# RWKV head norms: gate products made in the loop of the sums, and folded into the bonus and the heads

## The reference, cut to what matters

```python
g = jax.nn.sigmoid(xg @ g1) @ g2
...
mu = jnp.mean(y, axis=-1, keepdims=True)
var = jnp.mean(jnp.square(y - mu), axis=-1, keepdims=True)
y = ((y - mu) * lax.rsqrt(var + GN_EPS)).reshape(B, L, C)
y = y * ln_w.astype(f32) + ln_b.astype(f32)
bonus = jnp.sum(rh * kh * r_k.astype(f32), axis=-1, keepdims=True) * vh
y = y + bonus.reshape(B, L, C)
return (y.astype(h.dtype) * g) @ w_out
```

## Time and profile before

| | |
|---|---|
| median of 3 runs | 2298.06 us (2298.04 to 2304.33) |
| profiled execution, its own time | 2299.16 us |
| its span, first to last instruction | 2297.3 us |
| TensorE busy in the span | 2215.3 us (96%) |
| mean granted TensorE clock | 0.968 of full speed |
| VectorE, ScalarE, GpSimd busy | 1073.1, 804.6, 528.3 us |

### The profile page before, as it was taken

How to read it: one execution, slowest core, us unless ns; L and a number is a source line. 1 busy time by engine, 2 the same in 40 slices (tenths; PEclk the granted TensorE clock), 3 DMA queues, 4 the chain that set the end, 5 groups by cost and what they waited for, 6 DMA issues and landing times.

```text
span 2297.3 us, 50981 instructions
## 1 busy us (share of the span) xinstructions
PE 2215.3 (96%) x22812; PEld 1875.8 (82%) x22812; DVE 1073.1 (47%) x1480; ACT 804.6 (35%) x1388; POOL 528.3 (23%) x661
## 2 busy tenths in 40 slices
PE   7999998999899999899999999999998999999997
PEld 6888887877799955788888888888887668888886
DVE  5433325767566554743342463342274537433323
ACT  4333313574233341433332253332142324433320
POOL 2111103420233232621110331111162116211103
PEclk9999999999899997999999999999999779999999
DMA  4323321310000011232232132233123012323311
GB/s 159 129 93 117 118 79 56 113 67 19 13 4 4 4 56 70 102 107 96 93 130 91 56 108 96 93 113 127 56 70 106 1 37 74 111 93 114 130 51 37
DMA packets 28953, 183.42 MB, mean 80 GB/s; under 512 B 3216, under 2 KB 8144, under 8 KB 9792
## 3 DMA queue, kind: packets, MB, share of 16 engines
q1 hardware_dynamic: 27888, 178.79, 22.2%
q0 software_dynamic: 848, 1.37, 0.3%
HBM read 174.31 MB, written 4.30 MB: 78 GB/s over the span
## 4 chain that ended last, share of the span: by engine, by line
PE 87%; DVE 6%; POOL 3%; ACT 2%; issue 1%; DMA 0%; SPq 0%; POOLq 0%; ACTq 0%; DVEq 0%
PE psum L288 69%; PE psum L1603 6%; POOL h L348 1%; PE psum L1594 1%; PE psum L2470 1%; PE psum L2469 1%; PE psum L2456 1%; PE psum L363 1%; PE psum L1627 1%; POOL x L399 1%; DVE arena L340 1%; DVE split L263 1%; PE psum L1981 1%; PE psum L2301 1%; PE psum L1980 1%
## 5 line engine op out<-in xcount | busy, mean ns | idle before, releaser
L288 PE MATMUL psum<-x,split 128*128 128x256 f16 (+1 forms) x5568 | 642.6, 277 | 7.6 <-POOL x L399 6.1
L288 PEld LDWEIGHTS psum<-x,split 128*128 128x128 f16 x5568 | 544.9, 98 | 102.3 <-issue 16.0
L696 POOL TENSOR_TENSOR arena<-arena 128x256 f16<-128x256 f32 (+1 forms) x176 | 120.0, 682 | 772.7 <-ACT arena L545 772.7
L288 PE MATMUL psum<-x,split_more 128*128 128x256 f16 (+1 forms) x2496 | 288.2, 277 | 1.5 <-DVE x L2568 1.5
L288 PE MATMUL psum<-x,arena 128*128 128x256 f16 (+2 forms) x2448 | 281.9, 276 | 1.4 <-POOL x L947 1.2
L288 PEld LDWEIGHTS psum<-x,split_more 128*128 128x128 f16 x2496 | 245.8, 98 | 38.4 <-issue 1.9
L288 PEld LDWEIGHTS psum<-x,arena 128*128 128x128 f16 (+1 forms) x2448 | 240.7, 99 | 37.0 <-POOL x L947 2.5
L263 DVE SCALAR_TENSOR_TENSOR split<-stage,split 128x2048 f16<-128x2048 f32 (+1 forms) x77 | 190.5, 2474 | 161.1 <-ACT split L257 161.1
L288 PE MATMUL psum<-arena,split 128*128 128x256 f16 (+1 forms) x2304 | 260.9, 275 | 0.0
L288 PEld LDWEIGHTS psum<-arena,split 128*128 128x128 f16 x2304 | 225.0, 98 | 34.5 <-issue 2.2
L623 DVE SCALAR_TENSOR_TENSOR arena<-psum,arena 128x256 f32<-128x256 f32 (+1 forms) x176 | 75.4, 429 | 321.0 <-ACT arena L539 316.3
(11 more groups left out here) (217 smaller groups left out, 2652.6 us busy)
## 6 DMA issues: line engine op xcount, KB each, us to landing
stage<-in_w_gu SPq DMA_DIRECT2D x88, 1024.0 KB, 4.9
stage<-in_w_down SPq DMA_DIRECT2D x32, 1408.0 KB, 6.1
stage<-in_w_rkv SPq DMA_DIRECT2D x12, 1024.0 KB, 4.9
stage<-in_w_out SPq DMA_DIRECT2D x4, 1024.0 KB, 4.8
stage<-in_w_q SPq DMA_DIRECT2D x4, 1024.0 KB, 4.7
stage<-in_w_o SPq DMA_DIRECT2D x4, 1024.0 KB, 5.7
h_spill<-h SPq DMA_DIRECT2D x1, 2112.0 KB, 12.0
h<-h_spill SPq DMA_DIRECT2D x1, 2112.0 KB, 8.7
```

The lines of the kernel that those rows point to most:

```text
L288: last = pe.matmul(o, wt(wp, k), xs(xp, k), start=(k == 0 and wp == 0 and xp == 0), stop=(k == tiles - 1 and wp == 1))
L696: e.tensor_tensor(hid[s][:, 1, m, 0:n], hid32[:, no % 2, 0:n], hid[s][:, 0, m, 0:n], ALU.subtract).then_inc(hid_lo, 1)
```

## The change

The gates of all 16 tiles are made in the loop of the sums, ahead of bonus(i). As soon as tile i - 1 has its bonus and its square, DVE makes (bonus + ln_b) times gate and y times ln_w times gate (`with_gate`). What is left behind the inverse is one product and one sum (`normed`). FIRST = 11: from tile 11 on, the loop of the sums also makes inverse(i - 11) and normed(i - 11), so five tiles of half 0 are finished in the loop and three behind it. `inverted(1)` moves behind the norms of half 0. `split_hi` and `split_lo` of jobs[0] move forward to tiles 4 and 5; those of jobs[1] move behind the norms of half 0; those of jobs[2] and jobs[3] go between the groups of norms of half 1. The DMA that brings h back is cut in two: three quarters once all gates are made, the last quarter where it was; `s_back` is waited for at 32.

```diff
--- before.py
+++ after.py
@@ -833,7 +833,7 @@
                         beside.gpsimd(e, j)
                     sums(j, 0)
                 if beside:
-                    e.wait_ge(s_back, 16)
+                    e.wait_ge(s_back, 32)
                 add_h(e, T_out, 0)
                 sums(0, 1)
                 sums(1, 1)
@@ -1451,8 +1451,10 @@
                 gated.sync(e)
                 o.sync(e)
 
+                gated.gates_done(e)
+                e.dma_start(hflat[:, 0:6 * L], spill[:, 0:6 * L]).then_inc(s_back, 16)
                 gated.second.ready(e, KT - 1)
-                e.dma_start(hflat, spill).then_inc(s_back, 16)
+                e.dma_start(hflat[:, 6 * L:KT * L], spill[:, 6 * L:KT * L]).then_inc(s_back, 16)
 
             def act(e):
                 k_act(e)
@@ -1921,8 +1923,9 @@
             b_act, b_pool, b_pe, bon_dve = (sem(n) for n in ("rk_scaled", "rk_products", "bonus_sums", "bonus"))
             mean_pe, yc_dve, sq_act, var_pe = (sem(n) for n in ("y_means", "y_centred", "y_squares", "y_variances"))
             sd_act, sd_dve = sem("y_deviations"), sem("y_inverses")
-            gate_pe, iv_pe, yn_dve, y1_dve = (sem(n) for n in ("out_gates", "inverses_spread", "y_normed", "y_with_bonus"))
-            z_dve, z_act, z_pool = (sem(n) for n in ("gated", "gated_high", "gated_rest"))
+            gate_pe, bong_dve, yg_dve = (sem(n) for n in ("out_gates", "bonus_gated", "y_gated"))
+            iv_pe, yn_dve, z_dve, z_act, z_pool = (sem(n) for n in ("inverses_spread", "gated_normed", "gated_sums",
+                                                                     "gated_high", "gated_rest"))
 
             def t(arr, s, k):
                 a, m = HALF[s]
@@ -1958,44 +1961,52 @@
                     e.matmul(psum[0:HEADS, 4 + s, 0:width(s)], c("pick")[:, p0:p0 + HEADS], ysq[:, i % 2, 0:width(s)],
                              start=(k == 0), stop=(k == KT - 1)).then_inc(var_pe, 1)
 
+                def gate(i):
+                    s, k = tiles[i]
+                    a, m = HALF[s]
+                    if i >= 2:
+                        e.wait_ge(yg_dve, i - 1)
+                    e.matmul(at(i, 6 + i % 2), g2_sb[:, 0, k * P:(k + 1) * P], sgate[:, 0, a:a + m], start=True, stop=False)
+                    e.matmul(at(i, 6 + i % 2), g2_sb[0:GLO, 1, k * P:(k + 1) * P], sgate[0:GLO, 1, a:a + m], start=False,
+                             stop=True).then_inc(gate_pe, 1)
+
                 mean(0)
                 mean(1)
                 for i in range(2 * KT):
+                    gate(i)
                     bonus(i)
                     variance(i)
                     if i + 2 < 2 * KT:
                         mean(i + 2)
-                for i in range(KT):
-                    gate(e, i)
+                    if i >= FIRST:
+                        inverse(e, i - FIRST)
+                for i in range(2 * KT - FIRST, KT):
                     inverse(e, i)
 
-            def gate(e, i):
-                s, k = tiles[i]
-                a, m = HALF[s]
+            FIRST = 11
+
+            def inverse_bank(i):
                 if i >= KT:
-                    e.wait_ge(z_dve, i)
-                elif i >= 2:
-                    e.wait_ge(z_dve, i - 1)
-                o = at(i, 6 + i % 2 if s == 0 else 6)
-                e.matmul(o, g2_sb[:, 0, k * P:(k + 1) * P], sgate[:, 0, a:a + m], start=True, stop=False)
-                e.matmul(o, g2_sb[0:GLO, 1, k * P:(k + 1) * P], sgate[0:GLO, 1, a:a + m], start=False,
-                         stop=True).then_inc(gate_pe, 1)
+                    return 6 + i % 2
+                return 4 if i < 2 * KT - FIRST else i % 2
 
             def inverse(e, i):
                 s, k = tiles[i]
                 a, m = HALF[s]
                 e.wait_ge(sd_dve, s + 1)
-                if s == 0:
-                    if i >= 2:
-                        e.wait_ge(yn_dve, i - 1)
-                    else:
-                        e.wait_ge(bon_dve, 2 * KT)
-                e.matmul(at(i, i % 2 if s == 0 else 7), spreads[:, k * P:(k + 1) * P], sd[:, a:a + m], start=True,
+                if i == 2 * KT - FIRST:
+                    e.wait_ge(bon_dve, 2 * KT)
+                if i == KT:
+                    e.wait_ge(yg_dve, 2 * KT)
+                if 0 < i < 2 * KT - FIRST:
+                    e.wait_ge(yn_dve, i)
+                elif i % KT >= 2:
+                    e.wait_ge(yn_dve, i - 1)
+                e.matmul(at(i, inverse_bank(i)), spreads[:, k * P:(k + 1) * P], sd[:, a:a + m], start=True,
                          stop=True).then_inc(iv_pe, 1)
 
             def second_pe(e, q):
                 if q % 4 == 0 and q // 4 < KT:
-                    gate(e, KT + q // 4)
                     inverse(e, KT + q // 4)
 
             def act(e):
@@ -2026,14 +2037,16 @@
                     if i + 2 < 2 * KT:
                         scaled(i + 2)
                     square(i)
+                    if i == 4:
+                        split_hi(e, jobs[0])
                     if i == 8:
                         deviation(0)
-                    if i == 10:
-                        split_hi(e, jobs[0])
+                    if i >= FIRST + 1:
+                        high(e, i - FIRST - 1)
                 deviation(1)
+                for i in range(2 * KT - FIRST - 1, KT):
+                    high(e, i)
                 split_hi(e, jobs[1])
-                for i in range(KT):
-                    high(e, i)
                 split_hi(e, jobs[2])
 
             def high(e, i):
@@ -2057,45 +2070,53 @@
                     e.wait_ge(sd_act, s + 1)
                     e.reciprocal(sd[:, a:a + m], sd[:, a:a + m]).then_inc(sd_dve, 1)
 
+                def with_gate(i):
+                    s, k = tiles[i]
+                    y, bon, g = t(y_all, s, k), t(v_all, s, k), at(i, 6 + i % 2)
+                    e.wait_ge(gate_pe, i + 1)
+                    e.wait_ge(bon_dve, i + 1)
+                    e.scalar_tensor_tensor(out=bon, in0=bon, scalar=v("ln_b", k), in1=g, op0=ALU.add,
+                                           op1=ALU.mult).then_inc(bong_dve, 1)
+                    e.wait_ge(sq_act, i + 1)
+                    e.scalar_tensor_tensor(out=y, in0=y, scalar=v("ln_w", k), in1=g, op0=ALU.mult,
+                                           op1=ALU.mult).then_inc(yg_dve, 1)
+
                 for i, (s, k) in enumerate(tiles):
                     e.wait_ge(mean_pe, i + 1)
                     e.scalar_tensor_tensor(out=t(y_all, s, k), in0=at(i, 2 + i % 2), scalar=-1.0 / HD, in1=t(y_all, s, k),
                                            op0=ALU.mult, op1=ALU.add).then_inc(yc_dve, 1)
+                    if i:
+                        with_gate(i - 1)
                     e.wait_ge(b_pe, i + 1)
                     e.tensor_tensor(t(v_all, s, k), at(i, i % 2), t(v_all, s, k), ALU.mult).then_inc(bon_dve, 1)
+                    if i == 5:
+                        split_lo(e, jobs[0])
                     if i == 9:
                         inverted(0)
-                    if i == 11:
-                        split_lo(e, jobs[0])
-                for i in range(KT):
+                    if i >= FIRST:
+                        normed(e, i - FIRST)
+                with_gate(2 * KT - 1)
+                for i in range(2 * KT - FIRST, KT):
                     normed(e, i)
-                    if i == 1:
-                        inverted(1)
-                    if i == 3:
-                        split_lo(e, jobs[1])
-                split_lo(e, jobs[2])
+                inverted(1)
+                split_lo(e, jobs[1])
 
             def normed(e, i):
                 s, k = tiles[i]
-                yk, bon = t(y_all, s, k), t(v_all, s, k)
+                y, bon = t(y_all, s, k), t(v_all, s, k)
                 e.wait_ge(iv_pe, i + 1)
-                e.tensor_tensor(yk, yk, at(i, i % 2 if s == 0 else 7), ALU.mult).then_inc(yn_dve, 1)
+                e.wait_ge(yg_dve, i + 1)
+                e.tensor_tensor(y, y, at(i, inverse_bank(i)), ALU.mult).then_inc(yn_dve, 1)
                 e.wait_ge(yn_dve, i + 1)
-                e.scalar_tensor_tensor(out=bon, in0=yk, scalar=v("ln_w", k), in1=bon, op0=ALU.mult,
-                                       op1=ALU.add).then_inc(y1_dve, 1)
-                e.wait_ge(y1_dve, i + 1)
                 if i >= 3:
                     e.wait_ge(z_pool, i - 2)
-                e.wait_ge(gate_pe, i + 1)
-                e.scalar_tensor_tensor(out=zz[:, i % 3, 0:width(s)], in0=bon, scalar=v("ln_b", k),
-                                       in1=at(i, 6 + i % 2 if s == 0 else 6), op0=ALU.add, op1=ALU.mult).then_inc(z_dve, 1)
+                e.tensor_tensor(zz[:, i % 3, 0:width(s)], y, bon, ALU.add).then_inc(z_dve, 1)
 
             def second_dve(e, j):
                 if j < 2:
                     for i in range(4 * j, 4 * j + 4):
                         normed(e, KT + i)
-                if j == 0:
```

(12 more changed lines are left out.)

## The result

| | before | after |
|---|---|---|
| median | 2298.65 us (2298.04 to 2304.33, 5 runs) | 2287.22 us (2281.46 to 2289.36, 5 runs) |
| ratio, 95% interval | | 0.995, 0.9935 to 0.9964 |
| profiled execution | 2299.16 us, span 2297.3 | 2287.22 us, span 2285.3 |
| stage, from the first head mean to the eviction of out(3, 0) | 101.6 us | 90.4 us (820.2 to 910.6) |

The change is 11.4 us faster; 14.7 were forecast. A second set of runs of the same kernel gave 2286.99 against 2298.30, again 11.3. The profiled stage is shorter by 11.2, so nearly all of the difference arises in it: of the rest, the first head mean comes 1.6 us later in this profile, and what stands behind the stage takes 2.4 us less.

What follows compares the result with a forecast made beforehand. TensorE, 87% of the chain, bounds the kernel, mostly losing to half clock. Stage: 76.1 + 0.2 + 1.6 + 4.7 + 0.5 + 3.8 = 86.9 us against 101.6, 14.7 less: median 2283.4, range 2277.5 to 2290.5.

Steps and rivals of the forecast that it cites:

- The likeliest case: Whole kernel: the forecast itself, 14.7 us less, median 2283.4, own range 2279 to 2289, chance 0.65.
- Clock through the loop: Loop of the sums: gates among 128-row matmuls keep full clock; the old half-clock stretch, 16.2 us lost, goes.
- rival 1: New loop of the sums: the clock falls there; all 16 tiles at half cost 46 us, giving 2330; chance 0.06.
- Stalls of the loop: Loop of the sums: TensorE waits on the other engines' work, 1.6 us in all (0.5 to 3.5).
- The two inserts: Loop of the sums: `split_lo` at tile 5 stalls 0.5 us, the reciprocal at tile 9 0.3.
- Idle in the gap: Behind the loop: TensorE waits for DVE's norms and reciprocal before inverse(8), 4.7 us (3.5 to 6).
- Clock at the gap: Gap behind the loop and start of the projection: the clock surely falls, costing 3.8 us (1.4 to 7).
- Idle in the projection: Projection: 0.5 us, from norm 12 coming late; the earlier 3.3 us of idle goes.
- Opening: Start of the stage, at the first means: 0.2 us.
- The DMA that brings h back: Reload of h for POOL's adds: costs nothing, unless the 8 us of slack is gone.
- Matmuls: Whole stage: the same matmuls of the same sizes are issued, so 76.1 us at full clock stays.
- the fold: Norms: only a product and a sum left behind the inverse; in the projection DVE needs 0.85 us a tile, not 1.5.

Runs made afterwards that it cites:

- experiment 2: Kernel before, with only the second gate matmul and the inverse matmul reading 128 rows each, of other data; 9.2 us faster than before.
- experiment 1: Kernel before, plus two 128-row float32 filler matmuls behind each of the first half's eight gate-and-inverse pairs; 0.4 us faster than before, ratio 0.9988 to 1.0006.
- experiment 5: Changed kernel with its 16 inverse matmuls over 128 rows instead of 16, on other data; 15.7 us faster than the kernel before.
- experiment 9: Changed kernel with FIRST = 16, reciprocal behind norm 2, filler matmuls behind inverses 2 to 7; 3.5 us faster than the kernel before.
- experiment 3: Changed kernel with a third VectorE instruction, a copy of y onto itself, between each norm's product and sum; 6.4 us faster than the kernel before.
- experiment 4: Changed kernel with seven 128-row filler matmuls in the gap, one behind inverse(6), six behind inverse(7); 11.1 us faster than the kernel before.
- experiment 7: Changed kernel with the second half's reciprocal ahead of the first half's last three norms; 8.7 us faster than the kernel before.

## Why the prediction was right, and where its size was off

The likeliest case came true: full clock through the loop, one gap, one fall of the clock there. Point by point, forecast and measured:

- Clock through the loop: 1.00, as said; rival 1 did not happen. The half-clock stretch of the first half's norms was caused by gates and inverses standing alone, as argued: with the same matmuls at full rows (experiment 2) or with full ones between them (experiment 1) the clock held.
- Stalls of the loop: 1.6 forecast, 0.64 + 0.21 measured. The two inserts were right. The tiles from 11 on did not stall, because TensorE itself took 3.70; with the price that I had used for it (3.3) they would have: experiment 5, where it is nearly that, takes 3.48 a tile by the chain over DVE, for which 3.6 had been expected.
- Idle in the gap: 4.7 forecast, 0.17 + 0.92 + 3.36 = 4.45 measured in TensorE's timeline. That this is so near is in part luck: inverse(8) started 8.0 us after bonus(15) instead of 7.1, by the slow inverse(7) and the slow last sum, and the matmuls in between took 3.6 instead of 2.4.
- Clock at the gap: 3.8 forecast. 8.6 us at 0.50 are 4.3, and inverse(7) lost 0.6: 4.9. The fall was forecast from the length of the gap, but it came ahead of the long pause, at inverse(7), and experiments 5 and 9 point to the 16-row inverses as having a part in it.
- Idle in the projection: 0.5 forecast, none measured. Opening: 0.2 forecast, none measured.
- The DMA that brings h back, the splits and their loads: hidden, as said.

The step that was mis-sized is *Matmuls*: "so 76.1 stays". The instructions are the same, but their price depends on their neighbours. A 16-row inverse costs 0.46 us behind the 32-row matmul of a gate, as in the kernel before; behind a 128-row matmul it costs 0.65, and the 128-row matmul after it takes 0.63 instead of 0.43. The loop, from the first mean to the end of inverse(4), took 51.4 us: 48.7 by the forecast's prices, 0.85 of stalls, and 1.8 of this price. In the projection the five groups at full clock, each with the inverse behind it, make 5 x (2.12 - 1.83) = 1.5, with 0.43 + 1.40 = 1.83 for the inverse at 256 tokens and its group. The inverses of the gap and of the groups at half clock add some 0.8. Together 4.1 us; the smaller terms above give 0.6 back, and 3.5 is what the stage missed its forecast of 86.9 by. Experiment 5 took the price of the inverses away and the stage became 85.7, below the forecast, because the clock also came back sooner. In the loop it gained only 0.7 us, since DVE's chain then set the pace.

Held against the kernel before, the same terms give the 11.2 us, to rounding: 11.3 less lost to half clock (16.2 before, 4.9 now), 3.3 less of stalls in the loop (4.1, 0.85), 0.6 less idle (5.0, 4.45), 0.2 less at the opening, and 4.1 more for matmuls. The clock is the term that decides, as forecast.

The forecast gave the fold itself no term of its own beyond DVE's 0.85 instead of 1.5 a tile. Experiment 3 gives a size: 3.7 us for one instruction more behind the inverse, in one profile.

## What to carry to other kernels

When TensorE is busy all the time and its clock is at half, look at how many rows its matmuls have: here the clock was at half while each 128-row matmul was followed by one of 32 and one of 16 rows, and stayed full where more 128-row matmuls stood between them. So interleave stages instead of finishing one after the other. Price a short matmul by a row that has the same neighbours, not by one among its like. A gap of a few microseconds ahead of a dense stage can cost itself and a slow start of that stage besides; filler covered it in two experiments, and failed in the one where it stood behind the fall. Before trusting one stage's gain, look at the whole time as well: in experiment 4 the stage gained 4.7 us and the whole nothing.

## What the runs showed of the hardware

- The clock fell after TensorE had been busy 5.56 of 5.70 us and stayed at 0.50 while it was busy 16.20 of 16.20; it held at 1.00 with TensorE busy 13.49 of 19.00 when the same matmuls had full rows and other data (experiment 2).
- A float32 matmul of 16 rows and 272 columns between matmuls of 128 rows takes 0.65 us, one of 128 rows in the same place 0.47; with 256 columns and twelve float16 matmuls behind it 2.12 against 1.82.
- How soon the clock comes back varies between like places: 13.7 us at half in the changed kernel, 24 (4.5 in the gap and 19) in the one with the reciprocal first (experiment 7), though there TensorE never waited once the projection ran.
- The spread of whole runs (8 us in the changed kernel's) is as large as the effects sought; the stage in one profile shows where an edit acts, the medians whether it pays.
